# Seven block products for eight in a quarter of the gate/up products of a SwiGLU layer, with a deeper weight ring and the FFN in two halves

## What is computed

```python
h = rmsnorm(x, g_mix);  proj = h @ w_in          # then two attentions, gates, w_o_a, w_o_b, w_out
x = x + mixed @ w_out
h = rmsnorm(x, g_ffn)
x = x + (silu(h @ w_ffn_gate) * (h @ w_ffn_up)) @ w_ffn_down     # D_FF = 5632
h = rmsnorm(x, g_ple)
x = x + sigmoid(h @ w_ple_gate) * (p @ w_ple_proj)
return rmsnorm(x, g_final)
```

## Time and profile before

| | |
|---|---|
| median of 3 runs | 1481.36 (1480.99 to 1482.55) |
| span of the profiled execution | 1480.3 |
| PE busy, share of the span | 1461.7, 99% |
| DVE busy | 886.1, 60% |
| ACT busy | 694.3, 47% |
| HBM read | 275.87 MB, 188 GB/s |
| granted TensorE clock, mean | 0.999 |

### The profile page before, as it was taken

How to read it: one execution, slowest core, us unless ns; L and a number is a source line. 1 busy time by engine, 2 the same in 40 slices (tenths; PEclk the granted TensorE clock), 3 DMA queues, 4 the chain that set the end, 5 groups by cost and what they waited for, 6 DMA issues and landing times.

```text
span 1480.3 us, 19515 instructions
## 1 busy us (share of the span) xinstructions
PE 1461.7 (99%) x6846; PEld 1222.8 (83%) x6846; DVE 886.1 (60%) x1071; ACT 694.3 (47%) x857; POOL 62.1 (4%) x90
## 2 busy tenths in 40 slices
PE   7999999999999999999999999999999999999997
PEld 6888888888888888888888888888888888888886
DVE  6976776667655576565555555455554454554655
ACT  6544344544445455446444344444444444444544
POOL 4021001100210000000000000000000000000000
PEclk9999999999999999999999999999999999999999
DMA  7665565566555566666666666766666766666663
GB/s 198 203 191 170 176 195 174 167 176 204 175 168 165 159 235 227 216 217 216 211 206 207 206 194 201 212 207 209 204 207 183 219 207 193 210 199 200 227 203 124
DMA packets 183661, 290.91 MB, mean 197 GB/s; under 512 B 18808, under 2 KB 67888, under 8 KB 183344
## 3 DMA queue, kind: packets, MB, share of 16 engines
q1 hardware_dynamic: 173936, 281.52, 61.8%
q10 hardware_dynamic: 9664, 8.57, 2.0%
HBM read 275.87 MB, written 2.11 MB: 188 GB/s over the span
## 4 chain that ended last, share of the span: by engine, by line
PE 96%; DVE 2%; POOL 1%; DMA 1%; ACT 1%; issue 0%; ACTq 0%; DVEq 0%; POOLq 0%
PE acc L1360 52%; PE acc L1365 26%; PE acc L1239 8%; PE acc L1248 4%; PE side L1360 2%; PE side L1365 1%; DMA rope_c<-in_rope_rows 1%; DVE ls L771 0%; PE side L1406 0%; PE side L1412 0%; DVE ang_r L799 0%; POOL turn L405 0%; PE acc L1390 0%; PE acc L1389 0%; PE acc L1391 0%
## 5 line engine op out<-in xcount | busy, mean ns | idle before, releaser
L771 DVE TENSOR_TENSOR ls<-ws,hs 128x1024 fp32r<-128x1024 f32 x516 | 626.2, 1227 | 524.0 <-ACT hs L441 519.4
L441 ACT ACTIVATE hs<-ws 128x1024 fp32r<-128x1024 f32 x516 | 540.9, 1058 | 712.1 <-PE acc L1365 489.7
L1360 PE MATMUL acc<-hs,xg 128*128 128x512 f32 x1632 | 403.0, 389 | 0.0
L1360 PEld LDWEIGHTS acc<-hs,xg 128*128 128x128 f32 x1632 | 306.3, 188 | 63.6
L1365 PE MATMUL acc<-ls,xg 128*128 128x512 f32 x816 | 218.1, 389 | 0.0
L1365 PEld LDWEIGHTS acc<-ls,xg 128*128 128x128 f32 x816 | 153.2, 188 | 31.8
L1360 PE MATMUL acc<-hs,ff 128*128 128x512 f32 x704 | 173.9, 389 | 0.0
L1360 PE MATMUL acc<-hs,hn 128*128 128x512 f32 (+1 forms) x704 | 171.9, 387 | 0.0
L1360 PEld LDWEIGHTS acc<-hs,ff 128*128 128x128 f32 x704 | 132.1, 188 | 27.5
L1360 PEld LDWEIGHTS acc<-hs,hn 128*128 128x128 f32 x704 | 127.1, 188 | 24.2
L1239 PE MATMUL acc<-hn,hs 128*128 128x512 f32 x560 | 139.5, 393 | 1.1 <-DVE hn L811 0.7
(11 more groups left out here) (217 smaller groups left out, 856.5 us busy)
## 6 DMA issues: line engine op xcount, KB each, us to landing
ws<-in_w_in SPq DMA_DIRECT2D x152, 512.0 KB, 4.3
ws<-in_w_ffn_gate SPq DMA_DIRECT2D x88, 512.0 KB, 4.2
ws<-in_w_ffn_up SPq DMA_DIRECT2D x88, 512.0 KB, 4.4
ws<-in_w_ffn_down SPq DMA_DIRECT2D x88, 512.0 KB, 4.2
ws<-in_w_out SPq DMA_DIRECT2D x32, 512.0 KB, 4.7
ws<-in_w_ple_gate SPq DMA_DIRECT2D x32, 512.0 KB, 4.3
ws<-in_w_o_b SPq DMA_DIRECT2D x16, 512.0 KB, 4.3
ws<-in_w_o_a SPq DMA_DIRECT2D x16, 512.0 KB, 4.6
```

What stands on the lines that cost most here:

```text
L441: act.activation(hs[:, j, :], ws[:, j, :], ACT.Copy).then_inc(h_split, 1)
L771: dve.tensor_tensor(ls[:, j, :], ws[:, j, :], hs[:, j, :].bitcast(F32), ALU.subtract).then_inc(l_split, 1)
L1360: pe.matmul(banks[b], block_of(src, k, part, b), hs[:, slot, q * width:(q + 1) * width], start=first and q == 0 and part == 0, stop=False)
```

## The change

- **Block products.** For units 1 to 10, k-tiles 0 and 1 (group 0) and 2 and 3 (group 1) are taken together for gate and up at once, as a 2x2 block product: blocks of x are (k-tile, token block), blocks of W are (k-tile, gate or up). In place of eight products (24 matmuls) there are seven (21), by the Winograd form of Strassen's scheme. It needs four sums of x blocks for each group (made once, `xs`, in two parts), four sums of W blocks for each group and unit (DVE: `sums_1_3`, `sum_2`, `sum_4`, in f32, then split like weights), and sums of the results.
- **Pieces.** A unit has 20 pieces where it had 16 chunks: 2 plain gate, 4 of group 0 (a piece loaded; a piece loaded of which only the upper half is used; 2 pieces of sums), 4 plain gate, 4 of group 1, 6 plain up. The loads from HBM are still 16 for a unit. Matmuls: 12 x 12 + 2 x 21 = 186 for 192.
- **Results.** The seven products of both groups add up in `side` banks 0 to 3 and `acc` 0, 2, 3; the plain gate chunks add into `acc` 2, 3 and the plain up chunks into `acc` 0, 1. ACT copies one bank (`e_g` 0), DVE makes the combinations (`e_g`, `e_u`) and adds the plain parts.
- **Ring.** 12 slots of weights, 6 of high parts, and the low part is written over the weights (`l_ring` is `w_ring`). A load waits until the piece 12 earlier is used; a high part until the piece 6 earlier is used.
- **FFN in two halves.** Units 0 to 5, `w_ffn_down` for their rows (4 strips of 12 chunks, added to `x_tok`), units 6 to 10, `w_ffn_down` for the rest (4 strips of 10). `ff` is half as large. All of it is written out, without hardware loops.
- SP's eight moves stand behind other loads: in a unit behind piece 15, in the PLE stage behind piece 14.

```diff
+W_SLOTS, H_SLOTS = 12, 6
+HALVES = (6, N_FFN - 6)
+GROUPS = 2
+BLOCKS_AT = (2, 10)
+PLAIN, MIXED = 2 * K_CH, 2 * K_CH + 2 * GROUPS
# SP
+        def load_piece(i, src):
+            if i < SLOTS:
+                sp.wait_ge(l_split, C_FFN - SLOTS + i + 1)
+            elif i < 2 * SLOTS:
+                sp.wait_ge(chunk_used, C_FFN - 2 * SLOTS + i + 1)
+            else:
+                sp.wait_ge(chunk_used, C_FFN - W_SLOTS + i + 1)
...
+            load_up(i + 15, u, 3)
+            if u != HALVES[0]:
+                move_quads(sp, T_FF + u - 1, 0)
...
+                if n == 1 and c == 5:
                     move_quads(sp, T_PLE + N_WIDE - 1, 0)
# ACT, one unit
+            piece_highs(i + 6, 3)
+            if u != HALVES[0]:
+                move_quads(act, T_FF + u - 1, 1)
+            piece_high(i + 9)
+            if u != HALVES[0]:
+                ff_hi(u - 1)
+            blocks_high(u, 1)
+            piece_highs(i + 14, MIXED - 14)
+            act.wait_ge(chunk_used, C_FFN + i + 14)
+            act.wait_ge(ff_s, u)
+            act.activation(e_g[:, 0, :], side[:, 0, :], ACT.Copy).then_inc(e_first, 1)
+            next_highs(u)
+            act.wait_ge(gate_sum, u)
+            for b in range(2):
+                ins = act.activation(e_g[:, 2 * b, :], e_g[:, 2 * b, :], ACT.Silu, scale=rms[:, 0, 1, b:b + 1])
+            ins.then_inc(ff_silu, 1)
+            next_blocks(u)
# DVE, one unit
+            piece_low(i + 6)
+            sums_1_3(u, 1)
+            piece_low(i + 7)
+            sum_2(u, 1)
+            piece_low(i + 8)
+            sum_4(u, 1)
+            piece_low(i + 9)
+            if u != HALVES[0]:
+                ff_low(u - 1)
+            blocks_low(u, 1)
+            piece_lows(i + 13, MIXED - 13)
...
+            dve.tensor_tensor(e_g[:, 1, :], e_g[:, 0, :], side[:, 1, :], ALU.add).then_inc(e_step, 1)
+                sums_1_3(u + 1, 0)
+            dve.tensor_tensor(e_g[:, 2, :], e_g[:, 1, :], side[:, 2, :], ALU.add).then_inc(e_step, 1)
+                sum_2(u + 1, 0)
+            dve.tensor_tensor(e_u[:, :, :], e_g[:, 1:3, :], side[:, 3:4, :].broadcast_to([P, 2, WIDE]),
+                              ALU.subtract).then_inc(e_ready, 1)
+            piece_low(s)
+            dve.tensor_tensor(e_g[:, 0:3:2, :], e_g[:, 0:3:2, :], acc[:, 2:4, :], ALU.add).then_inc(gate_sum, 1)
+                sum_4(u + 1, 0)
+                piece_low(s + 1)
+                blocks_low(u + 1, 0)
+            up_result(u)
+            piece_low(s + 5)
# PE
+        def product(bank, x_h, x_l, i, half, start, stop):
+            at = slice(WIDE * half, WIDE * (half + 1))
+            w_h, w_l = h_ring[:, i % H_SLOTS, at], l_ring[:, i % W_SLOTS, at]
+            pe.wait_ge(h_split, C_FFN + i + 1)
+            pe.matmul(bank, x_h, w_h, start=start, stop=False)
+            pe.matmul(bank, x_l, w_h, start=False, stop=False)
+            pe.wait_ge(l_split, C_FFN + i + 1)
+            return pe.matmul(bank, x_h, w_l, start=False, stop=stop)
...
+            product(side[:, 0, :], *x_block(k, 0), i, 0, first, last)
+            product(acc[:, 2, :], *x_block(k + 1, 0), i, 1, False, last).then_inc(chunk_used, 1)
+            product(acc[:, 0, :], *x_sums(3, g), i + 1, 1, first, False).then_inc(chunk_used, 1)
+            product(side[:, 3, :], *x_sums(0, g), i + 2, 0, first, last)
+            product(side[:, 2, :], *x_sums(2, g), i + 2, 1, first, last).then_inc(chunk_used, 1)
+            product(side[:, 1, :], *x_sums(1, g), i + 3, 0, first, last)
+            product(acc[:, 3, :], *x_block(k + 1, 1), i + 3, 1, False, last).then_inc(chunk_used, 1)
```

More of the change, by code:

```diff
@@ new lines, in load_down @@
+        def load_down(half, n, c):
+            i, k = (I_DOWN_0, I_DOWN_1)[half] + DOWN_CH[half] * n + c, 4 * HALVES[0] * half + KW * c
+            load_piece(i, wdown_t[:, k:k + KW, WIDE * n:WIDE * (n + 1)])
+        for c in range(K_CH):
+            load_gate(c, 0, c)
+        move_quads(sp, T_FF - 1, 0)
+        for c in range(K_CH):
+            load_up(K_CH + c, 0, c)
+        for u in range(1, HALVES[0]):
+            load_unit(u)
+        for n in range(N_WIDE):
+            for c in range(DOWN_CH[0]):
+                load_down(0, n, c)
+                if n == 1 and c == 2:
+                    move_quads(sp, T_FF + HALVES[0] - 1, 0)
@@ L356, in _ @@
+        for u in range(HALVES[0], N_FFN):
+            load_unit(u)
+        for n in range(N_WIDE):
+            for c in range(DOWN_CH[1]):
+                load_down(1, n, c)
+                if n > 0 and c == 4:
+                    move_quads(sp, T_PLE - 2 + n, 0)
         for n in range(N_WIDE):
@@ L660, in _ @@
                 new_high(0, n - 1)
[L661 to L675, removed]
-            else:
[L677 to L681, removed]
+            if n < N_WIDE - 1:
+                split_chunks(C_OUT + 8 * n + 8, 4)
+            else:
+                piece_highs(0, 4)
@@ L695, in _ @@
[L695 to L698, removed]
+            next_blocks(u)
+        piece_highs(4, 2)
+        move_quads(act, T_FF - 1, 1)
+        piece_highs(6, 2)
+        squares(0, 3)
+        new_high(0, 3)
+        root(0)
+        piece_highs(8, 6)
+        act.wait_ge(rms_ready, 1)
+        act.wait_ge(chunk_used, C_FFN + K_CH)
+        for b in range(2):
+            ins = act.activation(silu_g[:, b, :], acc[:, 2 + b, :], ACT.Silu, scale=rms[:, 0, 1, b:b + 1])
@@ L1504, in _ @@
[L1504 to L1515 removed]
+        gate_banks, up_banks = pair_of(acc, 1), pair_of(acc, 0)
@@ new lines, in _ @@
+        pe.wait_ge(x_new, 3)
+        for c in range(K_CH):
+            pe.wait_ge(xg_ready, KW * (c + 1))
+            piece_by_token(c, tiles_of_chunk(c), xg, gate_banks, whole if c == 0 else going, c == K_CH - 1)
+        pe.wait_ge(x_new, 4)
+        for c in range(K_CH):
+            piece_by_token(K_CH + c, tiles_of_chunk(c), xg, up_banks, whole if c == 0 else going, c == K_CH - 1)
+        for u in range(1, HALVES[0]):
+            ff_unit(u)
+        strip_banks = [pair_of(side, 0), pair_of(side, 1), pair_of(acc, 1), pair_of(acc, 0)]
@@ new lines, in down @@
+        def down(half, done):
+            for n in range(N_WIDE):
+                if n < 2:
+                    pe.wait_ge(e_ready, done)
+                else:
+                    pe.wait_ge((gate_sum, up_sum)[n - 2], done)
+                for c in range(DOWN_CH[half]):
+                    if n == 0:
+                        pe.wait_ge(ff_ready, HALVES[0] * half + (KW * c + 1) // 4 + 1)
+                    i = (I_DOWN_0, I_DOWN_1)[half] + DOWN_CH[half] * n + c
+                    piece_by_token(i, tiles_of_chunk(c), ff, strip_banks[n], whole if c == 0 else going, c == DOWN_CH[half] - 1)
@@ L1517, in _ @@
+        down(0, HALVES[0] - 1)
+        for u in range(HALVES[0], N_FFN):
+            ff_unit(u)
+        down(1, N_FFN - 1)
         for n in range(N_WIDE):
```

448 lines of the change are left out of this document (331 added, 117 removed).

## The result

| | before | after |
|---|---|---|
| median (runs) | 1481.17 (4: 1479.53 to 1482.55) | 1465.24 (4: 1464.92 to 1466.90) |
| ratio, 95% interval | | 0.990 (0.9888 to 0.9912) |
| span of the profiled execution | 1480.3 | 1465.1 |
| first gate/up matmul of the FFN | 655.24 | 653.82 |
| from there to the end of the span | 825.06 | 811.28 |

The kernel is 15.9 us faster, 1.1%. The profiled execution of the changed kernel took 1466.90, 1.8 more than its span; this distance, 1.8 to 1.9 with spans given to 0.1, is the same in every execution of every kernel here.

The account below looks back on a forecast made before the run. TensorE, busy 99% of the span, was taken as the bound. Span 1480.3 - 13.6 for 60 matmuls + 0.4 PLE stall = 1467.1; with the median 1.06 above the span, 1468.2 us, range 1466.5 to 1475.4.

Parts of the forecast that it names:

- the bound, and what a matmul is worth: FFN stages: TensorE is the bound, each matmul removed gives 0.2267 us, 60 of them 13.60 us.
- the unit's layout: One mixed gate/up unit laid out in time over 42.16 us, closing without a wait of TensorE: cost 0.
- M: Time when all small moves have landed; in a unit at most 15.4, with TensorE waiting only beyond 17.7.
- The rival: DVE sets the units' pace: 37.8 us summed, decides from 42.2; at 20% above its sum 19 slower, 1500; chance 6%.
- waits (a): Some 20 more waits on TensorE in each unit, two on each product; taken as 0, at most 2 us in all.
- programs in straight lines (b): All engines' programs, now written out without loops, must be fetched; cost taken as 0.
- seams (c): Seams between gate/up units and the two down stages, where strips need `ff` in time; cost 0.
- the last step of the sum: From span 1467.1 to the runs' median, adding the 1.06 by which the median exceeded the span before: 1468.2 us.
- the head taken as unchanged: Stretch ahead of the first gate/up matmul of the FFN; the sum gave it no term.
- the PLE stall of 0.4: First PLE strip: TensorE waits for late moves, 0 to 1.1 us, taken as 0.4.
- the change gives more than the matmuls: Rival: a gain beyond the removed matmuls, from time in which PE isn't busy in these stages; chance 1%.
- E: End of the last down strip, from which the start of the PLE stage is timed; before, at 1373.34.

Follow-up runs that it names:

- a2_no_blocks: Changed kernel with its ring, halves and written-out loops, but all units plain with 192 matmuls, no block products; 1479.14 us.
- b4_moves_late: Changed kernel with SP's eight moves of each mixed unit behind the load of piece 17 in place of 15; 1471.78 us.
- b3_dve12: Changed kernel with twelve more dependent DVE adds of 512 columns in each mixed unit; 1488.79 us.
- a4_waits: Changed kernel with six more already satisfied TensorE waits on each of the 140 products, 840 in all; 1465.41 us.
- a3_unrolled: Kernel before with its FFN loops written out on all engines, nothing else; 1479.38 us.
- c1_unrolled_again: Kernel before with all FFN loops written out, the same edit as a3_unrolled run once more; 1479.50 us.
- c2 to c4: Kernel before with only some FFN loops written out: SP's 1480.72 us, PE's 1479.96, ACT's and DVE's 1480.78.
- d1: Changed kernel with two empty six-pass hardware loops added, one on DVE and one on PE, in the middle of the FFN; 1465.21 us.

## Why the prediction was right, and where it was not

**Right: the bound, and what a matmul is worth.** 13.62 less from the first gate/up matmul to the PLE stage for a forecast of 13.60, and a2_no_blocks puts 13.59 of it on the block products alone.

**Right: the unit's layout.** ACT's moves at 7.1 (forecast 7.1), SP's at 8.1 to 13.1 (8.2 to 13.4), M at 15.7 to 16.9 (at most 15.4, 0.3 to 1.5 short), the last step at 42.4 (42.4). The limit, laid out at 17.7, was 17.9 in b4_moves_late, where M went to 18.2 and beyond and the gain fell by 6.2.

**Right in direction, mis-sized: DVE.** 35.2 busy for a sum of 37.8. The single rows were right (1.22 for every form of 1024 columns; the 36 durations in a unit sum to 37.7), but instructions in a row overlap by some 0.08: eight low parts end 9.17 after the first began, so they follow each other every 1.14. On the other side, the point from which DVE decides was put at 42.2 of work and lies just under 41.0, since more than 1 us of waiting for ACT in each unit can't be filled. The two errors partly cancel: the reserve looked like 4.4 (42.2 - 37.8) and is a little under 5.8 (41.0 - 35.2). The rival's way to its price holds if that time is added: in b3_dve12 a full unit takes its DVE work + 1.2.

**Right: waits (a), programs in straight lines (b) and seams (c) at 0.** a4_waits for the first; for the others the rests 825.06, 825.10 and 824.87 of the kernels with loops, without, and with the new seams. On (b) the Trainium skill has a rule (Runtime: NRT & Kernel Launch, section "Instruction fetch mechanics"): a taken branch whose target lies outside the code at hand forces a fetch that the engine has to wait for. The rests show none of it in the FFN; whether it has a part in the open point below is not shown.

**Wrong: the last step of the sum, "the median of the runs lies 1.06 above the span of before; with the same distance", and the two terms beside it, the head taken as unchanged and the PLE stall of 0.4.** After, the median lies 0.1 above the span, the head is 1.42 shorter, and the stall is 0. The mechanism in the stages held; these terms make 2.7 of the 3.0 by which the sum missed. The range's low end allowed 1.3 for the spread of the runs, while the executions of the kernel before spread over 3.9. The rival "the change gives more than the matmuls" had 1%, for the reason that "the only reserve is the time in which PE isn't busy in these stages, and there is none". Inside these stages that is true to 0.2; the reason said nothing of the time outside them, and with all executions put together (below) the gain is 15.1, 1.5 more than the matmuls. By terms:

- *The PLE stall, 0.4: it is 0.* M came at E + 15.0, under the range of 16.1 to 17.7 that I had from two landings of 2.0 and 3.6 behind the last issue; here it was 1.3, and the issue ended 0.4 earlier than laid out. The Trainium skill's fixed 2.0 us for a DMA (DMA: Bandwidth & Descriptors, section "Anatomy of one DMA") had given no stall either, and there is none; but the section speaks of DMAs that GpSimd issues, and these come from SP and ACT and land 1.8 to 6.0 after issue. The landing of all these moves together went the other way, from a median of 1.9 to 3.2, and in the units the copy starts up to 3.9 behind the last issue. So the rows of other moves were a poor guide to this one.
- *The head, taken as unchanged: 1.42 shorter in the profiled execution.* No line of it was changed. TensorE's waits before 655 by what they were for, before and after:

```profile
PE acc L1248 <- DVE ls L771: 1.4, 2, 1.1
PE side L1283 <- DMA x_tok<-in_x: 1.4, 1, 1.4
```

```profile
PE acc L1589 <- DMA x_tok<-in_x: 0.6, 1, 0.6
PE acc L1554 <- DVE ls L935: 0.4, 1, 0.4
```

  These two waits together are 1.8 shorter: a load of `x`, and two low parts of weights. The timelines of TensorE show where (first the kernel before, then the changed one):

```profile
25.86 1.22 PE L1248 MATMUL acc<-hn,ls 128*128 128x256 f32 x8 [1.07 <-DVE ls L771]
53.40 2.08 PE L1248 MATMUL acc<-hn,ls 128*128 128x256 f32 x16
```

```profile
24.29 1.21 PE L1554 MATMUL acc<-hn,ls 128*128 128x256 f32 x8
51.81 2.08 PE L1554 MATMUL acc<-hn,ls 128*128 128x256 f32 x16
```

  These are the same matmuls of the two programs. The distance is 1.57 and 1.59, and 1.58 still at matmul 2500 (485.89 and 484.31). So these two heads part in their first 26 us; behind them only 0.16 changes. All sixteen profiled executions are alike in this: the head goes from 651.96 to 655.24 in the table, and matmul 250 starts between 51.89 and 54.59, while the stretch from there to the first gate/up matmul varies by only 0.9. For the changed kernel without an edit the head goes from 653.11 to 654.34. It scatters from execution to execution, and the profiled execution of before had the longest.
- *The 1.06 between span and median.* A time is its own span + 1.8. The 1.06 said only that the profiled execution of before was 0.7 over its median; after, where the profiled execution was the longest of four, it was 1.7 over. This makes 0.9 of the miss.
- *The rest.* 825.06 - 13.60 = 811.46 for 811.28 measured: 0.2, nearly all of it behind the last matmul. Other profiled executions of the kernel before, and of its forms with loops written out, have rests up to 825.42: in five of these six traces a matmul of the first unit comes 0.2 to 0.5 late, put down to the low part of `xg` (`new_low`, L1081), which follows the moves. None of the traces with the new ring has this; why not wasn't tested. The five of the changed kernel (with its controls and free waits) lie at 811.24 to 811.29, and a2_no_blocks, with the new ring, at 824.87. PE's busy share of 99% didn't show so short a stall.

0.4 + 1.4 + 0.9 + 0.2 = 2.9 of 3.0.

**What that leaves of the 15.9.** With all executions put together, the kernel before has a median of 1480.7 in 89 executions (1480.6 to 1480.7 beside each of the four groups, which ran on four chips), its form with all loops written out 1479.5 in 22, the changed kernel 1465.6 in 17 (its four kinds of run with no edit or with free waits). So 15.1 is the better value of the gain: 13.6 matmuls, 1.2 that came with the loops alone, and 0.3 left, about what the late matmul in the first unit took (this last was not tested). a2_no_blocks agrees: 1.6 of the 15.1 is there with all 192 matmuls in each unit. The 1.2 is a shift of shares: of the 89, 34 lie at 1478.6 to 1480.2 and 55 at 1480.4 to 1482.6, while of the 33 executions of plain units written out (a3_unrolled, c1_unrolled_again, a2_no_blocks) 3 lie above 1480.3. **Open:** why programs that are written out on all engines fall into the long group less often. Single engines (c2 to c4) and two empty loops (d1) don't settle it, and the head's code is the same. Most of the scatter arises in the first 55 us, between the two traces shown at TensorE's waits for `x` and for low parts; that late transfers are behind these waits is argued and was not tested by an edit.

## What to carry to other kernels

When one engine is busy for the whole of a stage, count its instructions: the removed ones were worth their pace to 0.02 us in 13.6, and everything else was a question of whether the other engines' fixed orders still close. For that, lay one period out in time, find the earliest limit (here M = 17.7, measured 17.9), and expect an engine to be the bound before its work fills the period (here at 41.0 of 42.16, some 3% early). Take the offset between span and time from the same execution, don't take the profiled execution for the median one, and let the range hold the scatter of that kernel's executions (here 3.9 us, 1478.6 to 1482.6), also when it is wider than every cost in the sum.

## What the runs showed of the hardware

- Executions of one kernel on one core fall in two loose groups 2 us apart (for the kernel before around 1479.1 and 1481.2), and the share of the long ones was smaller when the FFN's loops were written out. The FFN and PLE stages took the same time in a long execution (811.28, of 1466.90) and in a short one (811.24, of 1465.03).
- Four semaphore instructions of 51 ns within a product's 0.68 us (eight waits as written, all met) cost TensorE nothing; the unit stayed at 42.16.
- DVE's adds and subtracts of 1024 f32 columns take 1.22 with a broadcast, a strided, an in-place or a PSUM operand, and follow each other every 1.14.
- Eight small moves take 5.0 to be issued, and ACT, whose queue they are on, starts no copy meanwhile (788.72 and then 793.87, "issue" for 4.09 between them); the copy that needs them all started 1.3 to 3.9 behind the end of the issue.
